# Eight modulation tiles and the order of attention units in a two-layer fp32 kernel

## What is computed

```python
# first layer, 8 + 8 heads of 64, 2 + 2 key groups
kc_cmp, vc_cmp = compress(kc), compress(vc)            # 31 compressed keys
o_cmp = softmax(q_n @ kc_cmp) @ vc_cmp                 # "cmp"
o_sel = causal attention over the chosen 64-key blocks # "sel": with 8 blocks and top 16, all are chosen
o_win = causal attention in a window of 512            # "win": all earlier keys
score = sum_h relu(qi_h @ ki) * wi_h                   # index scores, 512 x 512
idx   = top_k(score, 128)
o_dsa = softmax over the keys of idx                   # "dsa"
x = x + concat((g0*o_cmp + g1*o_sel + g2*o_win) * silu(z_n), o_dsa * silu(z_d)) @ w_out
# second network, for each of two layers and two condition vectors c
m = silu(c) @ w_ada[i] + b_ada[i]                      # 9 * 1024 values: m[0] ... m[8]
h = ffn_half_step(h, g, m[0], m[1], m[2], w13, w2)     # m[2] only gates the result
h = mixer(h, m[3], m[4], m[5]); h = ffn_half_step(h, g, m[6], m[7], m[8], ...)
```

## Time and profile before

| what | us |
|---|---|
| runs before: median of 3 | 3452.81 |
| lowest and highest of them | 3432.56 and 3461.04 |
| the profiled execution: its time | 3457.02 |
| its span, first to last instruction | 3454.9 |
| TensorE's mean granted clock in it | 0.935 |

### The profile page before, as it was taken

One profiled execution on the slowest core, in us unless ns is written; L12 is line 12 of the kernel. 1 busy time (PEld: TensorE's weight loads), 2 busy tenths in 40 slices (PEclk: granted clock), 3 DMA queues, 4 the chain that ended last, 5 costly groups with the idle time before them and its releaser, 6 DMA issues. The chain is left out here.

```text
span 3454.9 us, 43440 instructions
## 1 busy us (share of the span) xinstructions
PE 3259.5 (94%) x18372; PEld 2819.4 (82%) x18372; DVE 1803.5 (52%) x2690; ACT 839.4 (24%) x1019; POOL 127.1 (4%) x96
## 2 busy tenths in 40 slices
PE   7847989899999999989999999999999999899999
PEld 6746878788888888668888888888888886699997
DVE  4656464276463663653644543664654556554434
ACT  3312222241121231222311212321211132132222
POOL 2320122000000000000000000000000000000000
PEclk9975555899999999999999999999999999999999
DMA  4332001234242412112333221343433320233331
GB/s 140 91 117 89 13 13 37 86 113 149 81 130 75 125 52 62 29 54 62 104 103 91 91 74 58 89 128 103 122 110 85 94 60 17 69 92 94 92 89 58
DMA packets 340322, 288.36 MB, mean 83 GB/s; under 512 B 12896, under 2 KB 315488, under 8 KB 339168
## 3 DMA queue, kind: packets, MB, share of 16 engines
q1 hardware_dynamic: 340192, 286.58, 28.3%
HBM read 279.72 MB, written 2.10 MB: 82 GB/s over the span
## 5 line engine op out<-in xcount | busy, mean ns | idle before, releaser
L2117 PE MATMUL PS<-x_hi_f,w_lo 128*128 128x258 f32 (+2 forms) x2560 | 622.3, 324 | 0.0
L2117 PE MATMUL PS<-x_lo_f,w_hi 128*128 128x258 f32 (+2 forms) x2560 | 622.0, 324 | 0.0
L2117 PE MATMUL PS<-x_hi_f,w_hi 128*128 128x258 f32 (+2 forms) x2560 | 620.9, 323 | 0.8 <-DVE w_lo L2165 0.8
L2117 PEld LDWEIGHTS PS<-x_hi_f,w_hi 128*128 128x128 f32 x2560 | 395.4, 189 | 43.9 <-issue 1.5
L2117 PEld LDWEIGHTS PS<-x_hi_f,w_lo 128*128 128x128 f32 x2560 | 395.3, 189 | 42.0
L2117 PEld LDWEIGHTS PS<-x_lo_f,w_hi 128*128 128x128 f32 x2560 | 393.2, 189 | 40.5
L2132 ACT ACTIVATE w_hi<-w_raw 128x2048 fp32r<-128x2048 f32 x131 | 250.0, 1909 | 498.6 <-PE PS L2117 496.7
L2117 PE MATMUL PS<-hid_hi_f,w_hi 128*128 128x512 f32 x1232 | 341.7, 347 | 0.9 <-DVE hid_lo_f L2185 0.9
L2117 PE MATMUL PS<-hid_hi_f,w_lo 128*128 128x512 f32 x1232 | 341.3, 347 | 0.0
L2117 PE MATMUL PS<-hid_lo_f,w_hi 128*128 128x512 f32 x1232 | 338.9, 345 | 0.0
L2165 DVE TENSOR_TENSOR w_lo<-w_raw,w_hi 128x2048 fp32r<-128x2048 f32 x131 | 299.6, 2287 | 35.1 <-ACT w_hi L2132 35.1
(11 more groups left out here) (325 smaller groups left out, 4607.1 us busy)
## 6 DMA issues: line engine op xcount, KB each, us to landing
w_raw<-in_w_ffn_dram SPq DMA_DIRECT2D x240, 512.0 KB, 5.1
sq_f<-in_w_ada_dram SPq DMA_DIRECT2D x120, 512.0 KB, 3.6
w_raw<-in_w_in_dram SPq DMA_DIRECT2D x46, 512.0 KB, 5.0
ada_room<-in_w_ada_dram SPq DMA_DIRECT2D x24, 512.0 KB, 3.5
w_raw<-in_w_out_dram SPq DMA_DIRECT2D x24, 512.0 KB, 5.2
w_raw<-in_w_ffn_dram SPq DMA_DIRECT2D x32, 384.0 KB, 3.9
ada_s<-in_conditions_dram SPq DMA_DIRECT2D x4, 1024.0 KB, 5.4
hT<-hT SPq DMA_DIRECT2D x56, 64.0 KB, 2.0
```

Source lines behind the costliest of these rows:

```text
L2117: last = nc.tensor.matmul(c.PS[:, 4 * q + 2 * w + m, 0:e - a], wt, xt[:, a:e], start=first, stop=end)
```

## The change

```diff
 compress, tensor engine, after the last product of the compressed values:
                 last.then_inc(out_done.sem, 1)
+                c.keep_warm(36, 7)
                 pe.wait_ge(normed.sem, 1)
 index_scores, tensor engine, after the loop:
+                c.keep_warm(14, 7)
 attend_first:
-    units = [FirstUnit(t, b) for t in range(QT - 1, -1, -1) for b in ("cmp", "sel", "win")] + [FirstUnit(t, "dsa") for t in range(QT)]
+    units = [FirstUnit(t, "cmp") for t in range(QT - 1, -1, -1)]
+    units += [FirstUnit(t, b) for t in range(QT - 1, -1, -1) for b in ("sel", "win")] + [FirstUnit(t, "dsa") for t in range(QT)]
-    rounds_at = [3, 8, 8, 2, 6, 6, 2, 4, 4, 1, 2, 2]
+    rounds_at = [0, 0, 0, 0, 9, 10, 6, 7, 4, 4, 4, 4]
-            for i in range(n_units):
-                share.load(sp, i)
                     row(i, j)
-                    keep_warm(4 + j % 4, True)
+                    for b in range(4, 8):
+                        keep_warm(b, True)
                     if u.branch == "cmp":
+                        if i >= 1:
+                            dve.wait_ge(maxed, row_first[i])
-                share.vector(dve, ch, i)
 AdaShare.finish:
-    def finish(self, dve, ch):
+    def finish(self, dve, ch, some=None):
-        dve.wait_ge(ada.done, self.tiles[-1].stop)
+        dve.wait_ge(ada.done, max(l * N_MOD * KT + (m + 1) * KT for l, m in which))
 first_block:
-            share = AdaShare(..., [2] * 8, [])
+            share = AdaShare(..., [2] * 8, [(0, 0), (0, 1)])
-                later = AdaShare(..., [0, 1, 1, 0, 1, 1, 0, 0, 0, 0, 0, 0, 1, 1, 1, 1], [(0, m) for m in range(3)], share)
 ffn, vector engine, after the tiles of a step:
                         share.vector(dve, c.dve.on(dve), s - s0)
+                        if soon and s - s0 == soon[0]:
+                            share.finish(dve, c.dve.on(dve), soon[1])
-def ada_shares(up, down):
+def ada_shares(up, down, first=None):
-        out += [up] * min(8, FT - f) + [down if f == 0 else 0] * (KT // 2)
+        out += [first if first and f == 0 else up] * min(8, FT - f) + [down if f == 0 else 0] * (KT // 2)
-ADA_PLAN = {(0, 0): (ada_shares(2, 1), [(0, m) for m in range(3, 9)]),
+ADA_PLAN = {(0, 0): (ada_shares(2, 1, 3), [(0, m) for m in range(3, 9)], (3, [(0, 2)])),
```

More of the change, by code:

```diff
@@ L1797, in vector @@
             dot.then_inc(ada.done, 1)
-    def finish(self, dve, ch):
+    def finish(self, dve, ch, some=None):
         ada, nc = self.ada, self.ada.nc
-        if not self.finish_list:
+        which = some or self.finish_list
+        if not which:
             return
         dve.wait_ge(ada.small_in, 32)
-        dve.wait_ge(ada.done, self.tiles[-1].stop)
-        mods = [(l, v, m) for l, m in self.finish_list for v in range(2)]
+        dve.wait_ge(ada.done, max(l * N_MOD * KT + (m + 1) * KT for l, m in which))
+        mods = [(l, v, m) for l, m in which for v in range(2)]
         at = lambda l, v, m: ada.c.mod[:, l, v, m * KT:(m + 1) * KT]
@@ L1836, in first_block @@
             s_c, room = sb2("ada_s", [P, 2, D]), sb2("ada_room", [P, 3, D])
-            share = AdaShare(c.ada, s_c, [room[:, 0], room[:, 1]], room[:, 2], [2] * 8, [])
+            share = AdaShare(c.ada, s_c, [room[:, 0], room[:, 1]], room[:, 2], [2] * 8, [(0, 0), (0, 1)])
             compress(c, T, KKc, KLc, Vc, dram, share)
@@ L1843, in first_block @@
             with scope(nc) as sb:
-                later = AdaShare(c.ada, s_c, share.bufs, share.product, [0, 1, 1, 0, 1, 1, 0, 0, 0, 0, 0, 0, 1, 1, 1, 1], [(0, m) for m in range(3)], share)
-                attend_first(c, sb, rows, O, Q, KK, KL, KKc, KLc, Vx, Vc, scores, sc_at, tri, dram, later)
+                attend_first(c, sb, rows, O, Q, KK, KL, KKc, KLc, Vx, Vc, scores, sc_at, tri, dram, share)
 class Refill:
@@ L1997, in invert, with ffn @@
         ch.link(self.c.nc.vector.reciprocal(self.inv[:], self.inv[:]))
-def ffn(c, sb, ring, x, w13, w2, gates, spans, tag, after=None, shares=None, finish=()):
+def ffn(c, sb, ring, x, w13, w2, gates, spans, tag, after=None, shares=None, finish=(), soon=None):
     nc = c.nc
```

## The result

| | us |
|---|---|
| before: median of 4 runs (lowest to highest) | 3442.68 (3427.49 to 3461.04) |
| after: median of 4 runs (lowest to highest) | 3492.16 (3471.25 to 3497.42) |
| ratio, 95% interval | 1.0141, 1.0096 to 1.0185 |
| profiled execution: span before, after | 3454.9, 3495.6 |

The time lies inside the predicted range and 12 us over the forecast. It is slower by more than 1%, which had a chance of 0.28. The spans differ by 40.7 us, where the steps of the prediction gave 27.

A forecast was written before the change was run, and what follows sets the result against it. Attention was taken as bound by PE at the low clock plus stalls on DVE, the ffn by PE with little DVE room. 3457.0 + 7.1 (attention) + 20 (ffn) = 3484, less 4.2 for the median: 3480 us, range 3446 to 3500.

The forecast's parts named there:

- part 5: First ffn: three tiles a step make weights wait on SP, steps of 19.1 us for 16.87, together +20 us.
- The rival of the hidden third tile: First ffn: weights land in time, so the third tile costs nothing; 3460 us, chance 0.10.
- part 3: Start of attention: four compressed units in a row, shaped like dsa 0, take 46.2 us, until 385.5.
- part 4: Attention after the compressed units: top-k rounds and stalls set unit lengths by a rule; attention ends at 630.7, 7.1 us later.
- The +7.1 us for attention: Whole attention: ends 7.1 us later, the units taking 291.4 us for 285.5; ends -6 and +13.
- parts 1 and 2: Before attention: spare matmuls bring no clock gain, the 14 delay the start 3.9 us; first score near 339.3, +1.2 us.
- part 2: Start of attention: also hangs on ACT's mask rounding and first copy_q, 335.4; first score 339.3, +1.2 us.
- That it stays up: Rival, attention: the clock stays high from the first compressed unit; 3382 us, chance 0.10.
- that sel 3 is fast: Rival, attention: the clock rises after the compressed units and holds until the first burst; 3466 us, chance 0.20.
- The last rival: Gaps in the ffn lower the clock too and late attention units take 49 us; 3491 us, chance 0.10.

The follow-up runs named there:

- e1_spread_tiles: Kernel after, with the moved tiles spread two to each up step and one to each down step of the first ffn: 3452.56 us, ratio 1.0037.
- e2_sp_order: Kernel after, still three tiles a step, with the third tile's load issued behind the next step's weights on SP: 3460.12 us, ratio 1.0097.
- e3_tiles_alone: Kernel before, with only the tile move: three in each of the first eight ffn steps, none in attention: 3438.58 us, ratio 1.0011.
- e4_before_spread: Kernel before, with only the tile move, the eight tiles spread over the ffn with no three in a step: 3419.26 us, ratio 0.9972.
- e5_no_dummies: Kernel after, without the 36 and 14 spare matmuls in compress and index_scores: 3493.25 us, ratio 1.0182.
- e7_dsa_burst: Kernel before, with 16 spare matmuls ahead of the first score of dsa 1: 3430.03 us, ratio 0.9995.
- e12_two_bursts: Kernel before, tiles moved and spread, compressed values padded to 128 rows, 16 spare matmuls each ahead of dsa 1 and the first selected unit: 3403.74 us, ratio 0.9880.
- e9_before_all: Kernel before, tiles moved and spread, compressed values padded to 128 rows, 16 spare matmuls ahead of dsa 1: 3410.36 us, ratio 0.9908.

## Why the prediction was right, and what it missed

- **The `ffn` (part 5): right.** +20 predicted; drain 1 to drain 9 takes 218.6 us for 198.5, +20.1. The chain came out by its terms: weights issued 8.1 us after the end of the step (7.8 predicted), landed and rounded 9.0 later (7.1 + 1.91), `w_lo` 2.29, a step of 19.3 for 19.1. e1_spread_tiles, e2_sp_order and e3_tiles_alone show the cause. The rival of the hidden third tile is out.
- **The four compressed units (part 3): the term that was mis-sized.** 46.2 predicted, 57.7 measured. I took dsa 0 as a unit of the same shape. Its `weigh` has 128 rows, theirs 32, and a pair of those holds up the next product by 0.34 us more (0.63 - 0.29). Eight pairs a unit are 2.7 of the 3.5 to 3.9 us that a unit was over; PE also idles 2.05 us in cmp 1 behind the late finish, for 0.9 in dsa 0. The weighing of cmp 0 falls into sel 3, which took 29.4 for 27.6 and 27.5 with full rows: 1.9 for four pairs, 0.48 for each, so that the 0.34 is rather too little and the shares within a unit stay open. 11.5 + 1.8, less the 0.8 by which attention began earlier, are 12.5 of the 13.0 by which it ended later than 630.7. The row that would have told it was there: sel 3 before is busy 29.60 of 29.60 us, 2 us over the rule of part 4, and it weighs cmp 3 in its first item.
  What a compressed unit takes also hangs on the clock and on what lies in it. Before, cmp 2 took 7.30 us with the clock partly high and only cmp 0 was long (windows of the kernel before):
```profile
405.40:412.70 7.30, 7.30 (x39) 5.95 (x38) 6.89 (x22) 2.81 (x5) 2.08 (x2) 0.73 0.00 0
...
506.40:521.10 14.70, 10.75 (x37) 8.01 (x37) 9.22 (x32) 2.81 (x5) 4.58 (x4) 0.50 0.00 0
```
  The +7.1 us for attention is the sum that failed in size: +20.1 was measured. It is the balance of two larger amounts, 10 us won by taking out the tiles and 29 lost by the order (e4_before_spread, e1_spread_tiles).
- **The top-k plan (part 4): right in its lengths, not in what they are made of.** Predicted against measured: win 3 28.6, 29.3; sel 2 24.4, 24.1; win 2 20.2, 20.8; sel 1 19.2, 19.2; win 1 16.2, 16.2; the three units ahead of dsa 1 45.0, 44.6; dsa 1 to 3 64.0, 64.0. PE's stall in win 3 is 2.27 us for 2.1. But the longest stalls in sel 2, win 2, sel 1 and win 1 are 5.33, none, 3.56 and 0.61 us for 4.3, 0.6, 5.7 and 2.7. Sel 2 came out right with part of it at the high clock (0.64), and sel 1 and win 1 because PE was busy 15.4 us in each where the rule had 13.5. The rule had split the old units wrongly: win 1 before is busy 15.46 of 16.30 us, so it idled 0.8 and not 2.7. That these lengths fit is in part luck, and no run isolates the rounds.
- **The spare matmuls (parts 1 and 2): right.** First score 338.5 for 339.3. The 3.9 us by which they hold up the start are 3.3 between e5_no_dummies and the kernel after; the total time of e5_no_dummies does not show them. The first `copy_q` on ACT is at 334.63 for 335.4. The start hangs on it, as part 2 has it.
- **The clock.** The prediction puts the low clock in slices 5 to 8; by the earlier trace rows the digits of 5 are slices 4 to 7, and the times given, 230 to 625 us, are about right. That it stays up, or that sel 3 is fast, did not come: 0.50 from 333.2 to 459.5 without a break. The last rival's number, 3491, is the one measured, but not by its mechanism: the `ffn` stood at 0.98 and the late units took 44.6, not 49. What the forecast did not know at all is that the last units can run at either clock from run to run. It counted them at 64.0 us in both kernels; the kernel before's median lies between its two groups, and three of the changed kernel's four runs lie in its upper one. With one clock in both the difference is 41 us, the 40.7 of the profiles, against 27 predicted. So that 3492 lies only 12 us over 3480 is in part luck: the forecast was counted from an execution of the upper group, and the measured median is of that group too.

The Trainium skill, "TensorE: Matmul & The Clock Gate", section "Why this matters for your kernels", has continuous busy time bring the full clock. The trace does not agree: sel 3, busy 29.40 of 29.40 us, stayed at 0.50, and the same unit ran at 1.00 in 16.0 us behind a burst of 16 spare matmuls. The same section has one matmul with 32 rows take the time of one with 128. These runs do not agree for pairs with 66 columns, of which one with 32 rows held up the next product by 0.63 us and one with 128 by 0.29.

## What to carry to other kernels

When work is added to a step, follow the queue that issues its loads, not only the engine that does it: a load that waits for a free slot holds everything behind it, and here it cost 20 us while DVE had room. When small units are put together, look for shapes that only they have, and at the clock that they had between the long units: here four of them went from 36 to 58 us, with wide rows of other units in them and the clock low throughout. When a change has two parts, run each alone; the balance of two large amounts is easily off by their difference. And before a change of a per cent is judged, look in several profiles for a stretch whose clock differs from run to run: 28 us of this kernel hung on three units, and 16 spare matmuls settled them in all 20 runs of two kernels.

## What was not expected of the hardware

- A `weigh` pair with a 32-row operand delays the next matmul by 0.63 us at the low clock, one with 128 rows by 0.29; the load of the former is not drawn ahead. Zeros to 128 rows made the compressed units and sel 3 some 24 us shorter, where the pairs account for 11 to 15 (32 x 0.34 or 0.48): the clock in the compressed units rose as well. The rest of the way from 3492.16 to 3442.95 us is the clock in dsa 1 to 3.
- The same busy unit ran at either clock: sel 3 29.4 us at 0.50 and 16.0 at 1.00; dsa 2 20.5 and 11.2. Busy time alone did not tell which, and in sel 3 of e7_dsa_burst the clock rose in its midst.
- e12_two_bursts, the best of all, is 27.4 us under the kernel before (3403.74 for 3431.13) with 32 spare matmuls, the padding and the tiles moved and spread. The 6.6 us that it has over e9_before_all are not shown to be its second burst's: the runs of the two overlap, and in the profiles the burst costs 4.4.
